# NSA layers: projection and compression in one stage, the pages of compression issued by GpSimd

## The reference, cut to what matters

```python
q, q_r, kc, vc, ks, vs, kw, vw, gates = nsa_project(h, w_in, pos)
kc_all, vc_all = full_seq(cache_cmp, kc, vc)          # samples: pages of the cache, then the new token
o_c, idx = nsa_compressed_select(q, kc_all, vc_all, pe, wc, pos)
o_s, o_w = nsa_local(qg, idx, pos, nsa_blocks(ks_all), nsa_blocks(vs_all), ...)
y = nsa_merge(o_c, o_s, o_w, gates, w_out)
```

## Time and profile before

| | us |
|---|---|
| median of three runs | 3682.13 (3681.27 to 3682.18) |
| the profiled execution | 3677.41 |
| its span | 3675.8 |
| first `nsa_project`, with its barrier | 12.8 to 195.0 |
| first `nsa_compress`, with its barrier | 195.0 to 320.2 |
| second of both | 2665 to 2974.7 |
| PE busy in the span | 3239.0 (88%) |
| DVE, ACT, POOL busy | 1870.1, 1262.5, 396.0 |

### The profile page before, as it was taken

How to read it: one execution, slowest core, us unless ns; L and a number is a source line. 1 busy time by engine, 2 the same in 40 slices (tenths; PEclk the granted TensorE clock), 3 DMA queues, 4 the chain that set the end, 5 groups by cost and what they waited for, 6 DMA issues and landing times. The chain is left out here.

```text
span 3675.8 us, 65936 instructions
## 1 busy us (share of the span) xinstructions
PE 3239.0 (88%) x25906; PEld 2993.7 (81%) x25906; DVE 1870.1 (51%) x3122; ACT 1262.5 (34%) x2150; POOL 396.0 (11%) x313
## 2 busy tenths in 40 slices
PE   6966888999889787878999898999989768889997
PEld 6764568999889787758999887999976745789997
DVE  4113654636479745345636484645451136446363
ACT  2103553423245332124323383423231035434232
POOL 2111211000034100020000131000031112100000
PEclk9978999999999899789999998999999889999999
DMA  3163513222222000123222323222232644032222
GB/s 133 70 219 115 159 38 131 86 98 83 77 64 83 19 0 0 63 80 143 89 95 77 92 79 110 92 89 96 63 106 98 192 131 156 30 131 83 92 86 66
DMA packets 136924, 341.21 MB, mean 93 GB/s; under 512 B 42856, under 2 KB 89576, under 8 KB 122488
## 3 DMA queue, kind: packets, MB, share of 16 engines
q1 hardware_dynamic: 112376, 279.25, 23.4%
q0 software_dynamic: 10496, 46.15, 3.7%
q10 hardware_dynamic: 13824, 12.59, 1.1%
HBM read 322.60 MB, written 32.12 MB: 96 GB/s over the span
## 5 line engine op out<-in xcount | busy, mean ns | idle before, releaser
L354 PE MATMUL ffn_ps<-ffn_x_hi_sb,ffn_w_hi_sb 128*128 128x260 f32 x2816 | 572.0, 284 | 40.3 <-DVE ffn_x_lo_sb L165 37.1
L354 PE MATMUL ffn_ps<-ffn_x_hi_sb,ffn_w_lo_sb 128*128 128x260 f32 x2816 | 570.0, 284 | 0.0
L354 PE MATMUL ffn_ps<-ffn_x_lo_sb,ffn_w_hi_sb 128*128 128x260 f32 x2816 | 569.5, 284 | 0.0
L354 PEld LDWEIGHTS ffn_ps<-ffn_x_hi_sb,ffn_w_hi_sb 128*128 128x128 f32 x2816 | 437.1, 190 | 44.9 <-issue 35.8
L354 PEld LDWEIGHTS ffn_ps<-ffn_x_hi_sb,ffn_w_lo_sb 128*128 128x128 f32 x2816 | 437.0, 190 | 0.0
L354 PEld LDWEIGHTS ffn_ps<-ffn_x_lo_sb,ffn_w_hi_sb 128*128 128x128 f32 x2816 | 436.0, 190 | 0.0
L394 ACT ACTIVATE ffn_w_hi_sb<-ffn_raw_sb 128x2048 fp32r<-128x2048 f32 (+2 forms) x152 | 256.8, 1689 | 349.0 <-PE ffn_ps L354 349.0
L446 DVE TENSOR_TENSOR ffn_w_lo_sb<-ffn_raw_sb,ffn_w_hi_sb 128x2048 fp32r<-128x2048 f32 (+2 forms) x152 | 304.8, 2005 | 47.3 <-ACT ffn_w_hi_sb L394 47.3
L412 ACT ACTIVATE ffn_pre_sb<-ffn_ps 128x520 f32<-128x520 f32 x176 | 106.5, 605 | 605.8 <-PE ffn_ps L354 317.1
L461 DVE SCALAR_TENSOR_TENSOR ffn_conv_sb<-ffn_pre_sb,ffn_conv_w_sb,ffn_conv_sb 128x512 f32<-128x512 f32 x176 | 132.3, 752 | 345.1 <-ACT ffn_conv_sb L414 345.1
L354 PE MATMUL ffn_ps<-ffn_inner_hi_sb,ffn_w_hi_sb 128*128 128x260 f32 x1408 | 283.9, 283 | 6.5 <-DVE ffn_inner_lo_sb L479 3.4
(11 more groups left out here) (446 smaller groups left out, 6276.4 us busy)
## 6 DMA issues: line engine op xcount, KB each, us to landing
ffn_raw_sb<-ffn_w_in SPq DMA_DIRECT2D x88, 1024.0 KB, 4.9
ffn_raw_sb<-ffn_w_out SPq DMA_DIRECT2D x32, 768.0 KB, 4.2
nsae_ring_sb<-sel_pages SPq DMA_DIRECT2D x160, 128.0 KB, 2.2
ffn_raw_sb<-ffn_w_out SPq DMA_DIRECT2D x32, 640.0 KB, 3.9
nsap_w_raw_sb<-nsa_w_in SPq DMA_DIRECT2D x32, 512.0 KB, 3.7
gdnp_w_raw_sb<-gdn_w_in SPq DMA_DIRECT2D x32, 512.0 KB, 3.7
nsac_pages_sb<-cmp_pages ACTq DMA_DIRECT2D x96, 128.0 KB, 3.7
nsac_pages_sb<-cmp_pages SPq DMA_DIRECT2D x96, 128.0 KB, 3.6
```

Source lines behind the costliest of these rows:

```text
L354: mm = pe.matmul(psf[:, bank + h, 0:H], wp[:, w[0], w[1]:w[1] + P], xp[:, h * H:(h + 1) * H], start=start and k == 0, stop=stop and k == 2)
```

## The change

One stage `nsa_base` (tensors named nsab) takes the place of both.

- The 16 tiles are projected in another order (the compressed keys and values first, then the selected ones, then the queries), with two weight slots for raw weights in place of three. The rotary swap is no matmul: ACT issues four transfers of 8 partitions each for a tile, and DVE multiplies what they bring.
- Compression is cut by sample: the prompt and then one sample at a time, 128 matmuls each. A matmul has a weight of 64 x 64 (no zeros), in one of four quarters of the array: 64 rows by the half of the head, 64 columns by head and by key or value. The prompt and sample 0 stand behind tile 4 of the projection, samples 1 to 5 behind tiles 6, 8, 10, 12 and 14 (counted from 0), samples 6 and 7 in the projection of the values.
- Pages come as 128 x 512 numbers (keys and values at once, 256 KB), 64 transfers a layer in place of 128. All are issued by POOL, four at a time, each four behind the `rest` of one weight as `pages_after` lists. Four numbers of pages are read by one instruction.
- Values and gates are projected as split parts with three products, in two passes of 8 steps (`v_step`) of 15 matmuls of 280 columns, among which the scores and softmax over compressed blocks are spread.
- SP issues the 32 ring transfers after the last compression, then the stores of the values. The loads in `nsa_attend` use the same unrolled form.

```diff
-    def load(self, sp, u, src):
+    def load(self, sp, u, src, cols=None, parts=None):
         if u >= self.raws:
             sp.wait_ge(self.lo_done, u - self.raws + 1)
-        sp.dma_start(self.raw[:, u % self.raws], src).then_inc(self.raw_in[u % self.raws], 16)
+        raw = self.raw[:, u % self.raws]
+        if parts:
+            raw = raw[:, 0:cols].rearrange("p (k c) -> p k c", k=parts)
+        sp.dma_start(raw, src).then_inc(self.raw_in[u % self.raws], 16)
...
+    order = [8, 9, 10, 11, 12, 13, 14, 15, 0, 1, 2, 3, 4, 5, 6, 7]
+    first_turn = 4
+    sample_after = {4: 0, 6: 1, 8: 2, 10: 3, 12: 4, 14: 5}
+    pages_after = {1: (0, 0), 2: (0, 1), 3: (1, 0), 4: (1, 1), 8: (2, 0), 9: (2, 1), 10: (3, 0), 11: (3, 1),
+                   12: (4, 0), 13: (4, 1), 14: (5, 0), 15: (5, 1), 16: (6, 0), 17: (6, 1), 18: (7, 0), 19: (7, 1)}
+    v_units = [(p, k0, n) for p in range(2) for k0, n in ((0, 3), (3, 3), (6, 2))]
     with ExitStack() as ctx:
...
+                    i = order[u]
+                    w.load(sp, u, d["nsa_w_in"][j, i // 2, :, i % 2 * KT * P:(i % 2 + 1) * KT * P])
+                else:
+                    p, k0, n = v_units[u - 16]
+                    c0 = VC * (1 - p)
+                    w.load(sp, u, d["nsa_w_v"][j, :, k0:k0 + n, c0:c0 + VC], n * VC, n)
+
+            sp.dma_start(v.table[:], d["page_table"]).then_inc(v.table_in, 16)
+            for u in range(22):
+                w_load(u)
+                if u == 1:
+                    sp.dma_start(pe_in[:], d["nsa_pe"][j]).then_inc(small_in, 16)
+                    sp.dma_start(rope[:], d["rope"]).then_inc(small_in, 16)
+                if u == 2:
+                    for kv in range(2):
+                        for g2 in range(2):
+                            half = slice(64 * g2, 64 * g2 + 64)
+                            sp.dma_start(w_cmp[half, kv], d["nsa_w_cmp"][j, half, kv, :, half]).then_inc(w_cmp_in, 16)
+                if u == 6:
+                    sp.wait_ge(copied, 4)
+                    sp.dma_start(o["nsa_kv"][j, :, 0:4], kv_c[:]).then_inc(stored, 16)
+                if u == 12:
+                    sp.wait_ge(rotated, 4)
+                    sp.dma_start(o["nsa_kv"][j, :, 4:8], v.kv[:]).then_inc(v.stored, 16)
+            sp.wait_ge(compressed, 9)
             for k in range(2):
-                sample_loads(sp, d, v, j, table, k, range(4), v.kv_in)
+                sample_loads(nc, sp, d, v, j, k, range(4), v.kv_in)
+            sp.wait_ge(v_copied, 10)
+            sp.dma_start(o["nsa_v"][j], v.vtn[:, 0:NCH]).then_inc(v.stored, 16)
+            sp.dma_start(o["nsa_v_new"][j], v.vtn[0:B, NCH]).then_inc(v.stored, 16)
+            sp.wait_ge(stored, 16)
+
+        @block.tensor
+        def _(pe):
+            norm.pe(pe, g.ones)
+
+            def compress(n, src, pages, cols):
...
+
+                views = by_page(src, pages)
+                if n:
+                    pe.wait_ge(cmp_copied, n)
+                for l in range(32):
+                    for kv in range(2):
+                        for g2 in range(2):
+                            rows = slice(64 * g2, 64 * g2 + 64)
+                            to = 64 * (g2 if kv == 0 else 1 - g2)
+                            mm = pe.matmul(ps[to:to + 64, 6 + g2, 0:cols], w_cmp[rows, kv, l, :], views[rows, kv, l],
+                                           start=(l == 0), stop=(l == 31))
+                mm.then_inc(compressed, 1)
+
+            def compress_prompt():
+                pe.wait_ge(w_cmp_in, 64)
+                pe.wait_ge(permuted, 1)
+                compress(0, prompt[:, :, :].rearrange("p t n -> p (t n)"), 5, 40)
+
+            def compress_sample(b):
+                pe.wait_ge(pages_in[b % 2], 16 * PAGES * (b // 2 + 1))
+                compress(b + 1, slots[b % 2], PAGES, 64)
+
+            for u in range(16):
+                if u >= 3:
+                    pe.wait_ge(copied, u - 2)
+                w.project(pe, u, lambda h: ps[:, 2 * (u % 3) + h, 0:H], norm).then_inc(projected, 1)
+                if u == 4:
+                    compress_prompt()
+                if u in sample_after:
...
+            def v_step(p, kt):
+
+                u, k = [(16 + m, kt - k0) for m, (q, k0, n) in enumerate(v_units) if q == p and k0 <= kt < k0 + n][0]
+                if k == 0:
+                    pe.wait_ge(w.lo_done, u + 1)
+                if p == 0 and kt == KT - 1:
+                    pe.wait_ge(padded, 1)
+                cols = slice(k * VC, (k + 1) * VC)
+                w_hi, w_lo = w.hi[:, u % 2, cols], w.lo[:, u % 2, cols]
+                for tt in range(5):
+                    if kt == 0:
+                        pe.wait_ge(*((copied, 16) if p == 0 else (v_copied, tt + 1)))
+                    at = kt * N + tt * P
+                    x = slice(at, at + P)
+                    out = ps[:, tt, 0:VC]
+                    pe.matmul(out, x_hi[:, x], w_hi, start=(kt == 0), stop=False)
+                    pe.matmul(out, x_hi[:, x], w_lo, start=False, stop=False)
+                    mm = pe.matmul(out, x_lo[:, x], w_hi, start=False, stop=(kt == KT - 1))
+                if u - 16 < 5 and kt + 1 == v_units[u - 15][1] or kt == KT - 1:
+                    mm.then_inc(projected, 1)
+
+            def c_scores(k):
+
+                if k:
+                    pe.wait_ge(c_stored, 1)
...
+            v_step(0, 0)
+            c_scores(0)
+            v_step(0, 1), v_step(0, 2)
+            c_scores(1)
+            v_step(0, 3)
+            c_tokens(0)
+            v_step(0, 4)
+            compress_sample(6)
+            c_tokens(1)
+            for kt in range(5, KT):
+                v_step(0, kt)
+            for kt in range(0, 3):
+                v_step(1, kt)
+            compress_sample(7)
+            v_step(1, 3)
+            s_scores()
+            cv_turns()
+            v_step(1, 4)
+            c_turns(0)
+            c_repeat()
+            v_step(1, 5)
...
+            def rope_swap(i, r):
+
+                act.wait_ge(copied, first_turn + r + 1)
+                if r >= 2:
+                    act.wait_ge(parted, r - 1)
+                else:
+                    act.wait_ge(zeroed, 1)
+                for base in (0, 64):
+                    for k in range(2):
+                        here, there = base + 8 * k, base + 8 - 8 * k
+                        act.dma_start(swap[here:here + 8, r % 2, :], raw(i)[there:there + 8, :]).then_inc(swapped[r % 2], 16)
+
...
+            def pages(b, half):
+                if b == 1 and half == 0:
+                    pool.wait_ge(norm.lo_done, KT)
+                if b >= 2 and half == 0:
+                    pool.wait_ge(compressed, b)
+                at = b * PAGES + 4 * half
+                _, ids = nc.values_load_multi_w_load_instructions(v.table[0:1, at:at + 4], engines=(pool.engine,),
+                                                                  min_val=0, max_val=N_PHYS - 1)
+                for p, page in enumerate(ids):
+                    to = (4 * half + p) * 512
+                    pool.dma_start(slots[b % 2][:, to:to + 512],
+                                 flat(d["cmp_pages"][j, bass.ds(page, 1)].rearrange("o p n -> p o n"))).then_inc(pages_in[b % 2], 16)
+
+            for x in (x_hi, x_lo):
+                ins = pool.memset(x[:, KT * N:].bitcast(F32), 0.0)
+            ins.then_inc(padded, 1)
+            w.rest(pool, 0)
+            pool.wait_ge(norm.summed, KT)
+            pool.memset(swap_flat, 0.0).then_inc(zeroed, 1)
+            for u in range(1, 22):
+                w.rest(pool, u)
+                if u == 1:
+                    pool.wait_ge(v.table_in, 16)
+                if u in pages_after:
+                    pages(*pages_after[u])
...
+            def rotate(i, r):
+                out = v.qr[:, i, :] if i < 8 else raw(i)
+                dve.wait_ge(swapped[r % 2], 64 * (r // 2 + 1))
+                if r:
+                    dve.wait_ge(rotated, r)
+                dve.tensor_tensor(part[:, :], swap[:, r % 2, :], rope[:, 1, :], ALU.mult).then_inc(parted, 1)
+                own.did(dve.tensor_tensor(out, raw(i), rope[:, 0, :], ALU.mult))
+                own.settle()
+                dve.wait_ge(parted, r + 1)
+                dve.tensor_tensor(out, out, part[:, :], ALU.add).then_inc(rotated, 1)
+
+            for u in range(first_turn, 16):
+                rotate(order[u], u - first_turn)
+
+            dve.wait_ge(rotated, 12)
+            own.did(dve.memset(keys_c[:].rearrange("p a g c -> p (a g c)"), 0.0))
```

## The result

The changed kernel takes 3621.67 us (median of 4 runs, 3614.92 to 3622.05) against 3681.7 before: ratio 0.9833, 95% interval 0.9816 to 0.985. 60 us (1.7%) are won where 99 were forecast. The direction and the range held. The time of a compression did not: something stops PE inside sixteen of the eighteen, and no row of before had shown it.

A forecast was written before the change was run, and what follows sets the result against it. Two stages bound by PE, with holes of 30 and 21 us, the second SP's ring issue. A layer's stage ends at 270.6 against 320.2, 49.6 saved, 99 in both: 3682.1 - 99 = 3583 us, range 3530 to 3660.

The forecast's parts named there:

- Direction and mechanism of the gain: Both NSA layers: swap matmuls go, tiles follow after 5.77 us, four quarters compress at once; chance of faster 0.89.
- the disputed size: Compression: 256 records a sample take 3.6 us with four quarters at once; the ends are 3.5 and 14.1.
- A: Rival on compression: only two quarters run at once, 7.1 us a sample, 3646 us in total; chance 0.17.
- B: Rival on compression: quarters run one after another, 14.1 us a sample, slower at 3772 us; chance 0.08.
- the estimate of 6.4 from a start floor: Compression: the skill's least start-to-start time of about 25 ns would give 256 x 0.025 = 6.4 us a sample.
- The end of tile 15: End of the first layer's projection with seven compressions, page waits and half clock, on the layer's clock: 196.9 us.
- Pages late: Before samples 2 to 5, PE waits 5.4 us for pages, four times: 21.6 us a layer.
- What these waits were worth: Each page wait before samples 2 to 5 costs 5.4 us idle plus 4.2 lost to half clock behind it.
- Rival C: No late pages: PE idles 2.7 us and the clock stays up, saving 27.6 more a layer: 3528 us; chance 0.12.
- First scores: Before the first scores over compressed blocks, PE stands 7.2 us until all rotations are done, put down to DVE.
- Ring: End of the stage: SP's 32 ring transfers take 27 us and end last, other engines idle the last 10 us.
- D: Rival: POOL is the bound, its rests and page waits grow; 3615 us, or 3643 with the ring at 41.35; chance 0.13.

## Why the prediction was right or wrong

- **Direction and mechanism of the gain: right.** Swaps gone, tiles 5.73 us apart (5.77 forecast), both holes of the earlier trace rows closed to one of 15 us, four quarters at once. The pace of quarters, the disputed size, was 0.0145 us a record, so 3.7 us a sample by itself, against 3.6. A and B fell.
- **The step that failed: "I take 3.6 us" for a compression as PE meets it.** A compression takes 3.7 us plus a stop for instructions. In the first layer the gap to the forecast is 290.6 less 270.6, 20.0 us; the stops between weight loads of a compression (the row above, 15.3, counts from the ends of the multiplies) add up to 16.4 (1.57, 1.57, 4.20, 1.90, 0.71, 1.97, 3.37, 1.13), to 17.9 in the second layer. At no place had I asked what a record costs besides PE's time. Sample 1 as PE met it (5.5 us at full clock) lay not far below rival A's 7.1 and the estimate of 6.4 from a start floor, but for another reason than either; a total time near A's would have looked like A by luck.
- **The rest of the 20.** The end of tile 15 came at 206.0, forecast 196.9. There: stops 11.9, a wait of 1.9 for ACT to empty the banks behind the prompt's compression (unforeseen), tiles and page waits 1.7 more; against them the first tiles 3.3 earlier, and records and half clock together 39.0 where 25.2 + 16.8 = 42.0 stood. From there to the last compression 52.5 for 44.3: stops 4.5; 17 us at half clock, some 8 lost where 4 stood; 0.9 for ACT's copy of tile 15, which I hadn't counted; and 1.9 less at the first scores. ACT's emptying of the first pass was 2.2 for the 2 that stood. From there on 32.1 for 29.4: 1.9 pass before SP begins the ring, and the issue is 1.0 longer.
- **Pages late: right in the sum, by two errors that cancel.** Waits of 5.7, 5.9, 5.8 and 5.0 us, 22.4 for 21.6. The issue was shorter (2.15 for 4.0), the landing longer (4.9 for 3.0).
- **What these waits were worth: wrong.** They had to be worth 5.4 + 4.2 each; taking them away gave 32 us in both stages, not 77: the stops grew in their place (by 6.3 and 9.8 us), and in the first layer 34 of the 37 us at half clock stayed. Rival C counted on that gain and would have failed in the same way.
- **First scores: right in kind, two us too long.** The wait is there and put down to DVE, 5.05 us by the row and 5.3 between the weight loads, for 7.2. Behind it weight loads stand 1.7 us more, but that is no wait of PE: the eight records of the scores take 1.9 us there.
- **Ring: right.** 27.97 us for 27, SP last, PE idle for 15 us at the end (10 forecast). The 27 was picked between 11 and 41, so its closeness is partly luck.
- **D: half right.** POOL's rests were not what PE waited for, and the rest of the weight took 2.3 to 2.4 us as before. But pages on POOL's queue did cost time, in a place that D did not name: 34 us lie between POOL's and SP's pages once neither is late. How much of it is the queue and how much the time of landing is open.

## What to carry to other kernels

PE's work has a second price besides its time: its instructions. Here 256 of them take 3.0 to 4.1 us from block to block in the kernel without pages (one 5.4), and 4.0 to 7.7 beside page traffic in the changed one, so a dense run of tiny matmuls (0.0145 us a record, load and multiply being two instructions) outruns it after a block or so; put such runs in pieces between long matmuls, but in few pieces, since each turn costs about a third of a us. In a profile the sign is idle time put down to "issue" inside one uniform group, at distances of whole blocks. And when a wait goes, ask what had been happening under its cover: removing it pays in full only if nothing else was being caught up there.

## What the runs showed of the hardware

- PE ran out of instructions: stops of 0.7 to 4.2 us in the first layer, all at 193 past a multiple of 256 recorded PE instructions, each ended 1.2 to 1.6 us behind the end of a 16 KB instruction packet.
- The fetch was slower beside other traffic: block to block 3.6 us with the DMA engines nearly idle and 6.1 at a share of 0.83 to 0.99, same sample and same block. Beside SP's pages at such a share it was 4.5. The packet itself took about 1 us each time; it started 1.0 us behind the crossing with the engines nearly idle and 3.4 with POOL's pages.
- Four 64 x 64 quarters at once give a record each 0.0145 us at a clock of 1.00.
- Going from 128 x 128 records to 64 x 64 and back costs about 0.34 us: rounds of 1.66 us for 1.31 of records; eight rounds cost 2.9 us in another kernel. Five rounds fewer in each of twelve tiles won 10 us, with some 5 taken back by stops.
- Stops of up to 2.5 us mostly left the granted clock at 1.00 (2.4 GHz); stops of 3 us and more and the page waits of 5 to 6 us were followed by 3.4 to 13.7 us at 0.50 (1.2 GHz).
